# Expert weights in wider rows, lists gathered as rows, and both output halves of an expert ended together

## The reference

```python
def swiglu(u, w_gu, w_down):
    g, up = jnp.split(u @ w_gu, 2, axis=-1)
    return (jax.nn.silu(g) * up) @ w_down
...
    for e in range(N_EXPERTS):
        out = out + combine[..., e:e + 1] * swiglu(u, w_gu[e], w_down[e]).astype(F32)
```

## Time and profile before

| | |
|---|---|
| median of 3 executions | 2103.68 us |
| the profiled execution, its own time | 2097.01 us |
| span of the profiled execution | 2095.3 us |
| first matmul of the first expert | 1250.19 us into the span |
| one expert, from gather to gather | 103.22 us |

### The profile page before, as it was taken

How to read it: one execution, slowest core, us unless ns; L and a number is a source line. 1 busy time by engine, 2 the same in 40 slices (tenths; PEclk the granted TensorE clock), 3 DMA queues, 4 the chain that set the end, 5 groups by cost and what they waited for, 6 DMA issues and landing times. The chain is left out here.

```text
span 2095.3 us, 25935 instructions
## 1 busy us (share of the span) xinstructions
PE 1872.8 (89%) x9774; PEld 1597.9 (76%) x9774; DVE 1425.4 (68%) x1524; ACT 1024.5 (49%) x1202; POOL 156.4 (7%) x137
## 2 busy tenths in 40 slices
PE   7889887689999995999966759999999999999996
PEld 2567665577887874787945649898989898989895
DVE  1685455455554555675458448988888888888887
ACT  3443243342222223322344337777676767676765
POOL 1241021000000000000058000000000000000000
PEclk9989898899999998899988869999999999999998
DMA  6444200243343442344400049999999999999994
GB/s 245 161 171 141 70 1 0 81 139 143 121 154 130 158 151 101 129 149 155 147 15 1 1 134 319 338 335 329 338 339 324 346 325 345 327 345 325 347 325 166
DMA packets 245889, 412.28 MB, mean 197 GB/s; under 512 B 7690, under 2 KB 161458, under 8 KB 245693
## 3 DMA queue, kind: packets, MB, share of 16 engines
q1 hardware_dynamic: 244472, 411.26, 57.2%
q10 hardware_dynamic: 1350, 0.11, 0.1%
HBM read 410.30 MB, written 1.05 MB: 196 GB/s over the span
## 5 line engine op out<-in xcount | busy, mean ns | idle before, releaser
L2295 DVE TENSOR_TENSOR w_low<-e_ring,w_high 128x1408 fp32r<-128x1408 f32 (+2 forms) x384 | 617.2, 1621 | 103.6 <-ACT w_high L2232 100.6
L2232 ACT ACTIVATE w_high<-e_ring 128x1408 fp32r<-128x1408 f32 (+2 forms) x384 | 528.6, 1382 | 215.7 <-PE ps L2145 213.1
L2143 PE MATMUL ps<-w_high,list_h 128*128 128x352 f32 x1024 | 338.3, 330 | 18.0 <-DVE w_low L2295 16.4
L2145 PE MATMUL ps<-w_high,list_l 128*128 128x352 f32 x1024 | 329.9, 322 | 0.0
L2144 PE MATMUL ps<-w_low,list_h 128*128 128x352 f32 x1024 | 329.3, 322 | 0.0
L2143 PEld LDWEIGHTS ps<-w_high,list_h 128*128 128x128 f32 x1024 | 192.9, 188 | 26.6 <-DVE w_low L2295 25.7
L1440 ACT ACTIVATE fw_high<-ring 128x1024 fp32r<-128x1024 f32 x66 | 70.0, 1060 | 278.4 <-PE ps L1389 188.3
L1474 DVE TENSOR_TENSOR fw_low<-ring,fw_high 128x1024 fp32r<-128x1024 f32 x66 | 80.8, 1225 | 175.1 <-ACT fw_high L1440 175.1
L2144 PEld LDWEIGHTS ps<-w_low,list_h 128*128 128x128 f32 x1024 | 193.8, 189 | 0.4
L2145 PEld LDWEIGHTS ps<-w_high,list_l 128*128 128x128 f32 x1024 | 192.6, 188 | 0.0
L1387 PE MATMUL ps<-u_high,fw_high 128*128 128x512 f32 x352 | 140.4, 399 | 6.9 <-DVE fw_low L1474 6.9
(11 more groups left out here) (366 smaller groups left out, 3519.0 us busy)
## 6 DMA issues: line engine op xcount, KB each, us to landing
e_ring<-in_e_w_gu_dram SPq DMA_DIRECT2D x128, 1408.0 KB, 8.0
e_ring<-in_e_w_down_dram SPq DMA_DIRECT2D x32, 1536.0 KB, 6.9
e_ring<-in_e_w_down_dram SPq DMA_DIRECT2D x32, 1280.0 KB, 7.7
bg_area<-in_mod_w_dram SPq DMA_DIRECT2D x72, 512.0 KB, 4.1
ring<-in_f_w_gu_dram SPq DMA_DIRECT2D x22, 1024.0 KB, 7.0
ring<-in_h_w_in_dram SPq DMA_DIRECT2D x10, 2048.0 KB, 8.1
ring<-in_m_w_in_dram SPq DMA_DIRECT2D x6, 2048.0 KB, 9.6
ring<-in_f_w_down_dram SPq DMA_DIRECT2D x5, 2048.0 KB, 7.7
```

The costliest lines, as they stand in the source:

```text
L2143: nc.tensor.matmul(out, high[:, f, :], w_high[:, c, :], start=(f == 0), stop=False)
L2145: last = nc.tensor.matmul(out, low[:, f, :], w_high[:, c, :], start=False, stop=(f == total - 1))
L2232: nc.scalar.activation(piece(k.w_high, p), raw(p), ACT.Copy).then_inc(S.high_done, 1)
L2295: nc.vector.tensor_tensor(piece(k.w_low, p), raw(p), piece(k.w_high, p).bitcast(F32), ALU.subtract).then_inc(S.low_done, 1)
```

## The change

What it does, part by part:

- **Units.** The up columns are cut into tiles of 512, 512, 512, 512, 384 and 384 columns. A unit holds both tiles of a pair (1024 or 768 columns, rows of 4096 or 3072 bytes) of one side, and 3, 3, 2 (or 4, 4) row blocks of it. Its two pieces are the two tiles of the pair. The down units are 3 row blocks x 1024 columns (the last one 1 row block), and their two pieces are the two output halves. There are 24 units and 48 pieces as before; pieces are 3, 3, 3, 3, 2, 2 row blocks for each side of the first two pairs, 4 for all 8 of the third pair, and 3 (14 of them) and 1 (the last 2) in the down part.
- **Ring.** The ring is placed under the last mixer's output stage, and SP loads the first four units there. In the expert loop SP loads unit j+4 of this or the next expert, and in the last expert four units that nobody uses; SP waits for these at the end.
- **Splits.** Splits 0 to 2 of the first expert come ahead of the loop, those of the next expert at p = 45 to 47, without a condition.
- **Lists.** `routing` splits the normed tokens into `tok_high` and `tok_low`. `gather` (after p = 20) is 8 matmuls of 512 columns giving the list as rows; ACT copies the two banks (`list_rows`, p = 21), and PE transposes them (`turn_list`, after p = 24), before `take` at p = 25.
- **Outputs.** Both halves end with the last piece. At the top of the next expert come `y_high` and `y_low` twice, then scatter of half 0 after p = 3 and of half 1 after p = 6; the adds stand at p = 4 and p = 7. Each scatter waits until the adds of the one before it have emptied its banks (`S.added`), as before.
- `turn_hidden` follows the six tiles; its places and some others move by a piece or so. The number table `slot_no` grows from 256 to 384 columns. Buffers change place.

The diff, cut to its core ("..." marks what is left out):

```diff
 
 E_RING = 4
-E_N = 352
-E_TILES = FFN // E_N
 E_SLOT = 6 * HALF
-E_UNITS = 2 * E_TILES + 2 * 4
+E_COLS = ((0, 512), (512, 512), (1024, 512), (1536, 512), (2048, 384), (2432, 384))
+E_CHUNKS = ((3, 3, 2), (3, 3, 2), (4, 4))
+E_UP_UNITS = tuple((pair, side, sum(E_CHUNKS[pair][:u]), m)
+                   for pair in range(3) for side in range(2) for u, m in enumerate(E_CHUNKS[pair]))
+E_DOWN_UNITS = tuple((f, min(3, FC - f)) for f in range(0, FC, 3))
+E_UNITS = len(E_UP_UNITS) + len(E_DOWN_UNITS)
 E_BUFS = 3
 E_PIECE = 3 * HALF
 LEVELS = 7
...
             s.send(sp, u0 + 2 + RING)
+            if column_major:
+                load_expert_unit(k, sp, 0, 3)
+                sp.wait_ge(w.low_done, 4)
+                load_expert_unit(k, sp, 0, 0)
+                sp.wait_ge(w.low_done, 8)
+                load_expert_unit(k, sp, 0, 1)
+                load_expert_unit(k, sp, 0, 2)
 
...
         def _(act):
+            for i in range(2):
+                nc.scalar.activation(k.tok_high[:, i, :], k.tok[:, 2 + i, :], ACT.Copy).then_inc(parts, 1)
...
+            for i in range(2):
+                dve.wait_ge(parts, i + 1)
+                nc.vector.tensor_tensor(k.tok_low[:, i, :], k.tok[:, 2 + i, :], k.tok_high[:, i, :].bitcast(F32), ALU.subtract)
...
+def load_expert_unit(k, sp, e, j):
+
+    slot = k.e_ring[:, (j % E_RING) * E_SLOT:(j % E_RING + 1) * E_SLOT]
+    if j < len(E_UP_UNITS):
+        pair, side, c, m = E_UP_UNITS[j]
+        first, n = E_COLS[2 * pair][0], 2 * E_COLS[2 * pair][1]
+        src = k.a["e_w_gu"][0, e][c * P:(c + m) * P, side * FFN + first:side * FFN + first + n]
+    else:
+        (f, m), n = E_DOWN_UNITS[j - len(E_UP_UNITS)], D
+        src = k.a["e_w_down"][0, e][f * P:(f + m) * P, :]
+    sp.dma_start(slot[:, 0:m * n].rearrange("p (c n) -> p c n", c=m), src.rearrange("(c p) n -> p c n", p=P)).then_inc(k.e_loaded[j % E_RING], 16)
 
...
+    HIDDEN_TURNS = (13, 15, 25, 28, 34, 36)
...
+            def units(it, e, following):
+
+                for j in range(E_RING, E_UNITS + E_RING):
+                    need = sp.snap(it * PIECES + (2 * j + 2))
+                    sp.wait_ge(S.low_done, need)
+                    load_expert_unit(k, sp, e if j < E_UNITS else following, j % E_UNITS)
+
             with sp.Fori(0, n) as ps_:
-                with sp.Fori(0, EXPERTS) as e:
-                    it = sp.snap(ps_ * EXPERTS + e)
-                    gu = a["e_w_gu"][0, e]
-                    dn = a["e_w_down"][0, e]
-                    for j in range(E_UNITS):
-                        if j < Y0:
-                            t, side = j // 2, j % 2
...
+                for half in range(2):
+                    cols = slice(half * HALF, (half + 1) * HALF)
+                    for i in range(2):
+                        nc.tensor.matmul(k.ps[:, 4 + half, :], k.places[:, i, :], k.tok_high[:, i, cols], start=(i == 0), stop=False)
+                        last = nc.tensor.matmul(k.ps[:, 4 + half, :], k.places[:, i, :], k.tok_low[:, i, cols],
+                                                start=False, stop=(i == 1))
+                last.then_inc(S.gathered, 1)
+
+            def turn_list(m):
+
+                pe.wait_ge(S.rows_copied, 2 * m + 2)
                 for c in range(KD):
-                    for i in range(2):
-                        last = nc.tensor.matmul(k.ps[:, 4 + c // 4, (c % 4) * P:(c % 4 + 1) * P],
-                                                k.tok[:, 2 + i, c * P:(c + 1) * P], k.places[:, i, :],
-                                                start=(i == 0), stop=(i == 1))
-                last.then_inc(S.gathered, 1)
-
-            def three_passes(it, p, out, high, low, first, chunks, total):
+                    last = nc.tensor.transpose(k.ps[:, 4 + c // 4, (c % 4) * P:(c % 4 + 1) * P], k.list_rows[:, c * P:(c + 1) * P],
+                                               k.ident[:, :])
...
+                    def follow(p):
                         if p == 3:
-                            scatter(ys + 1, adds, 1)
-                        elif p == 11:
+                            scatter(ys + 1, adds, 0)
+                        elif p == 6:
+                            scatter(ys + 2, adds + 2, 1)
+                        elif p == 10:
                             turn_places(it, adds, e)
-                        elif p == 21:
+                        elif p == 20:
 
                             gather(ps_ * 9 + e + 1)
+                        elif p == 24:
+                            turn_list(ps_ * 9 + e + 1)
...
-
...
+                    for p in range(Y0):
+                        pair, side, c, m = E_UP_UNITS[p // 2]
+                        b = p % 2
+                        if c == 0:
+                            pe.wait_ge(S.hid_done if side else S.silu_ready, it * TILES + 2 * pair + b + 1)
+                        three_passes(it, p, k.ps[:, 2 * b + side, 0:width_of(p)], k.list_h, k.list_l, KD)
+                        follow(p)
 
...
+                    for p in range(Y0, PIECES):
+                        f, m = chunks_of(p)
+                        if p % 2 == 0:
+                            pe.wait_ge(S.hid_low, it * TILES + 1 + max(t for t in range(TILES) if rows_of_tile(t)[0] < f + m))
+                        three_passes(it, p, k.ps[:, 4 + p % 2, :], k.hid_h, k.hid_l, FC)
+                        follow(p)
+                scatter(ps_ * 18 + 17, ps_ * 36 + 32, 0)
+                scatter(ps_ * 18 + 18, ps_ * 36 + 34, 1)
...
+            def list_rows(m):
+                act.wait_ge(S.gathered, m + 1)
+                for half in range(2):
+                    nc.scalar.activation(k.list_rows[:, half * HALF:(half + 1) * HALF], k.ps[:, 4 + half, :], ACT.Copy).then_inc(S.rows_copied, 1)
...
+            for p in range(E_BUFS):
+                split(0, p)
             with act.Fori(0, n) as ps_:
...
                 act.wait_ge(S.pcleared, ps_ + 1)
                 with act.Fori(0, EXPERTS) as e:
                     it = ps_ * EXPERTS + e
-                    for p in range(E_BUFS):
-                        split(it, p)
-                    act.wait_ge(S.gathered, ps_ * 9 + e + 1)
-                    y_high(it * PIECES, 1)
+                    act.wait_ge(S.list_turned, ps_ * 9 + e + 1)
+                    for half in range(2):
+                        y_high(it * PIECES, half)
                     for p in range(PIECES):
-                        if p + E_BUFS < PIECES:
-                            split(it, p + E_BUFS)
-                        if p < 2 * Y0 and p % 4 == 1:
-                            silu(it, p // 4)
...
+                        if p == 21:
+                            list_rows(ps_ * 9 + e + 1)
...
-                        if p == 39:
-                            act.wait_ge(S.pcopied, it + 1)
-                            y_high(it * PIECES + 40, 0)
-                y_high(ps_ * (EXPERTS * PIECES) + EXPERTS * PIECES, 1)
+                for half in range(2):
+                    y_high(ps_ * (EXPERTS * PIECES) + EXPERTS * PIECES, half)
...
+            find(0, 0)
+            for p in range(E_BUFS):
+                split(0, p)
             with dve.Fori(0, n) as ps_:
...
+                    for half in range(2):
+                        y_low(ys + 1 + half, half)
...
-                        if p == 13:
+                            add(adds, 0)
+                        if p == 7:
+                            add(adds + 2, 1)
...
-                        if p == 22:
+                        if p == 25:
...
-                        if p == 40:
-                            y_low(ys + 2, 0)
-                        if p == 43:
-                            add(adds + 2, 0)
-                y_low(ps_ * 17 + 17, 1)
-                add(ps_ * 34 + 32, 1)
+                for half in range(2):
+                    y_low(ps_ * 18 + 17 + half, half)
+                for half in range(2):
+                    add(ps_ * 36 + 32 + 2 * half, half)
+                find(ps_ + 1, 0)
 
...
+        def place_ring():
+
+            assert E_RING * E_SLOT == RING * SLOT + 4 * D
+            k.e_ring = at("e_ring", E_RING * E_SLOT, 2 * KD * T)
+            k.e_loaded = [sem(f"e_loaded{i}") for i in range(E_RING)]
...
-            lambda: mixer_out(k, "ho", "h_out", (2, 3), 96, k.g_cols, True, False),
+            lambda: (place_ring(), mixer_out(k, "ho", "h_out", (2, 3), 96, k.g_cols, True, False)),
```

More of the change, by code:

```diff
@@ L2339, in _ @@
                     it = ps_ * EXPERTS + e
-                    ys, adds = ps_ * 17 + 2 * e, ps_ * 34 + 4 * e
-                    for p in range(E_BUFS):
-                        split(it, p)
-                    y_low(ys + 1, 1)
+                    ys, adds = ps_ * 18 + 2 * e, ps_ * 36 + 4 * e
+                    for half in range(2):
+                        y_low(ys + 1 + half, half)
                     for p in range(PIECES):
-                        if p + E_BUFS < PIECES:
-                            split(it, p + E_BUFS)
```

(28 more changed lines are left out.)

190 lines of the change are left out of this document (87 added, 103 removed).

## The result

The change made the kernel slower: 2124.79 us in the median of four executions (2124.25 to 2136.42) against 2102.20 for four of the kernel before, ratio 1.0117, 95% interval 1.0084 to 1.0150 (here and below a ratio is not exactly the quotient of the two medians). The profiled execution took 2124.25 us, its span is 2122.5 us; before it was 2097.01 and 2095.3. In the first batch of the experiments two executions of the kernel before took 4499.52 and 5132.87 us; no median or ratio here counts them.

A forecast was written before the change was run, and what follows sets the result against it. PE was taken to pace the expert loop, the full ring hiding DMA. The terms summed to +33.5 us on 2097.0, 2130.5; with the median 6.7 above, about 2137. Range 2122 to 2145 (chance 0.55), wider 2105 to 2156.

The forecast's parts named there:

- matmuls and gather: Expert loop: wider matmul columns and gathering lists as rows save PE 1.55 us per expert, 12.4 us in all.
- boundary: Between experts: the short last pieces leave PE standing 2.3 us for split 0; net +1.95 at 7 boundaries, +13.7 us.
- late piece 3: Behind each boundary: split 3 comes late after three splits, a table load and two `y_high`; +0.8 each, +5.6 us.
- second scatter: After piece 6: PE stands 1.5 us for the first scatter's adds, which follow split 7 on DVE; +12 us over 8.
- other waits: Rest of an expert (short pieces, `take`, pushed splits): waits of 4.4 us for 3.4 before; +8 us, bounds 0 and 14.
- clock: PE's clock falls after the idle time at two of 7 boundaries, 1.7 us each; +3.4 us, bounds 0 and 12.
- head: Before the loop: token split, gather, copies, table load and first splits sum to +0.5 us, bounds -3 and +3.
- tail: After the last expert: second scatter behind the first adds, +2.2, and a `find` of 0.5; +2.7 us.
- Rival A: Whole kernel: DMA is the real pace, hidden in the splits' waits, so wide rows gain; about 2079 us; chance 0.11.
- Rival B: Expert loop: new waits are not additive, those behind the boundary shrink to nothing; +8, 2112 us; chance 0.15.
- C: Rival: every boundary drops PE's clock, and the scatter's wait comes on top; 2150 us; chance 0.12.
- D: Rival: prefetch gives the head its whole transfer time, boundary-following waits shrink to nothing; no change, 2104 us; chance 0.07.

The follow-up runs named there:

- run with 2, 2: The changed kernel with the down units cut 3 x 6, 2, 2 row blocks instead of 3 x 7, 1: 2115.92 us, ratio 1.0090.

## Why the prediction was right, and where its steps were off

The direction, its cause (waits at short pieces and late buffers that cost more than the matmuls gain) and the range held; 2137 was 12 us too high. Half of that is not a matter of the change: I had added 6.7 us because the median before stood that far above its profiled execution, and after the change it stood 0.5 above. From one profiled execution to the other the kernel became 27.2 us slower for a forecast of 33.5.

Even so part of the agreement is luck. For the loop I had 30.3 us and it took 16.1 more; at the end, where I had 2.7, it took 8.4 more, by a cost that I had not seen. With the end as I forecast it, the median would have been about 2119, below the 2122 to 2145 that I gave the best chance, and the run without the unneeded splits, at 2117.91, is there. The terms, from the forecast's sum to what the profile shows:

| term | forecast | shown |
|---|---|---|
| matmuls and gather | -12.4 | about -10 |
| boundary | +13.7 | +13.5 |
| late piece 3 | +5.6 | about +1; hidden behind the boundary |
| second scatter | +12 | +10.3 |
| other waits | +8 | -5 |
| clock | +3.4 | about +6 |
| head | +0.5 | +0.9 |
| tail | +2.7 | +8.4 |

The first six rows on the right come to about 16, as the loop's 16.1 us. They are losses read from PE's timeline, times the number of experts that show them.

**Matmuls.** 384 columns take 0.174 us, 512 take 0.227, as read. The losses that I can see sum to 5.7 us in an expert of 105.1 against 2.6 in one of 103.2, so the work proper fell by 1.2, not 1.55. That the gather is about 0.8 of it is shown by the run with the old gather; the part of the wider tiles was not tried by itself.

**Boundary.** The loss was 2.17 us for a forecast of 2.3 at seven places; before the change it was 0.24. A slow restart follows in both. The run with 2, 2 took off 1.40 for 1.37, and the short unit put first carried the wait with it to piece 34. So it is shown that the cover sets the wait.

**Piece 3.** I added this wait to the boundary's, though both are met by the same chain: while PE stands at the boundary, ACT and DVE work on. The run with the short unit first has no boundary wait and 1.38 us lost here; the run with 2, 2 has 0.77 at the boundary and up to 1.20 here; the changed kernel has 2.17 and at most 0.43. Terms that follow each other within a few pieces are not a sum.

**Second scatter.** The loss was 1.29 us for a forecast of 1.5, and it went when the add was moved; a third of it came back before piece 8.

**Other waits.** Here the working was weakest: 13 us off, and of the wrong sign. I had 4.4 us in an expert for 3.4 before, and the timelines show about 1.8 for 2.3; the 3.4 was what a sum of prices left over, not a reading. Before piece 29 the loss was 0.61 where I had 1.6 for `take`; before the change it had been 1.21, with 0.83 at another place. That the transposes after piece 28 cover it now is argued, not tried. Pieces 20, 30 and 37, for which I had 1.1, lost less than 0.1 together. Pieces 12, 18 and 24 came nearly as worked out (0.11, 0.35 and 0.81 for 0.28, 0.49 and 0.93), and moving the short pieces under other work took the last two away.

**Clock.** Four of seven boundaries show the fall. Stretches before and behind the boundary at 1464 us:

```profile
1461.70:1464.40 2.70, 0.69 (x3) 0.27 (x3) 2.07 (x2) 2.70 (x3) 0.00 (x0) 1.00 1.01 388
1464.40:1467.80 3.40, 3.40 (x9) 2.63 (x9) 3.40 (x3) 3.19 (x4) 0.00 (x0) 0.50 1.00 394
```

I had two falls at 1.7 us (3.4 us at half the clock). It was four, and such an expert took 1.0 us more, 106.1 for 105.1. But the 105.1 hold 0.43 us of loss before piece 3, and the 106.1 hold none, as PE is slow while that split is made: so a fall costs 1.4 us by itself, which is what the table counts. The number of falls in seven boundaries was four to six in all profiled runs with the 2.01 us gap except the one with the old gather, so this term is uncertain by some 3 us. The Trainium skill (TensorE: Matmul & The Clock Gate, The HAM clock gate) has the clock at 1.2 GHz after PE has been idle; the trace agrees that it falls to 0.50, but with the same 2.01 us of idle time it fell at four of seven boundaries here and at one of seven with the old gather. Why is open.

**Tail.** The other terms were mis-sized; here a cost was missed altogether. I counted the second half behind the first, +2.2, and a `find`, and did not see that splits 0 to 2 are issued on ACT and DVE behind the last expert too, ahead of `y_high` and `y_low`. The diff removes the condition that held them back. The run that puts it back ends 6.3 us earlier, with the clock at 1.00 for the scatters. The 2.1 us that are left over the kernel before are what I had priced at 2.7.

**DMA.** 0, as forecast. SP waited 740 us for slots, and rows of half the width changed nothing. Rival A (2079) falls. The Trainium skill (DMA: Bandwidth & Descriptors, Why small descriptors are slow) has a fixed overhead on each packet, by which, as an estimate, wide rows save a few per cent of the transfers' time; no run here shows that in the kernel's time (1.0117 with rows of 4096 bytes, 1.0115 with 2048), as the ring is full. Rival B (2112) had the waits behind the boundary shrink to nothing: the one before piece 3 nearly did, the one at the second scatter did not. C's fall at every boundary did not come (four of seven), and D (no change) fails on the same waits as B.

## What to carry to other kernels

Where one engine feeds on pieces that others prepare a fixed number of buffers ahead, compare the preparing time of a piece with what the engine has to do in the pieces between: a piece shorter than the rest makes a long one behind it late. Put short pieces where the engine has other work, and what empties a buffer ahead of the next preparation in the queue. When a condition for the last turn of a loop is dropped, see what stands behind it in each queue at the end. A wait hidden by a larger one comes out when that one is mended, as it did here before pieces 3 and 8.

## What I had not expected of the hardware

At equal idle time before it, 2.01 us, PE's clock fell to 0.50 at some boundaries and not at others (4 of 7 and 1 of 7 in two runs with the same gap), and once in the run with the short unit first, behind the idle time in the middle of an expert. A table load of 1.28 us on ACT stands at the top of the loop body although only copies stand on either side of it: before the change in front of split 0, after it in front of `y_high`:

```profile
1566.90 4.23 ACT L2277 ACTIVATE w_high<-e_ring 128x1536 fp32r<-128x1536 f32 x3 [1.41 <-PE ps L2190]
1571.15 1.28 ACT L2297 ACT_TABLE_LOAD   x1
1572.45 1.27 ACT L2297 ACTIVATE ey_high<-ps,ex 128x512 fp32r<-128x512 f32 x2
```

Three activations of 1.49 us take 4.23 together: back to back they overlap by about 0.1 us each, so the three splits end 0.24 us earlier than I worked out.
